# The last hidden block of both feed-forward stages in buffers of its own, and accumulator banks opened by a flag

## The chip, the cores and the metric

One Trainium2 chip, one of its cores. The time is the device time of one execution in microseconds: 890.45 us is the median of 3 runs (890.37 to 890.51). The inputs are drawn once; nothing is computed on the host.

## The reference

A block of three stages and then two attention layers, on 256 tokens of width 1024, all in float32. What the change touches is the feed-forward stage, which comes twice in the first block (`f` = 0 and `f` = 1):

```python
def swiglu(n, w_gate, w_up, w_down):
    return (jax.nn.silu(n @ w_gate) * (n @ w_up)) @ w_down

mod = (jax.nn.silu(c) @ w_ada[l] + b_ada[l])[:, None, :]
sh1, sc1, gt1, sh2, sc2, gt2, sh3, sc3, gt3 = jnp.split(mod, N_MOD, axis=-1)
n = modulate(rmsnorm(h, g_ffn1[l]), sh1, sc1)
h = h + 0.5 * gt1 * swiglu(n, w1_gate[l], w1_up[l], w1_down[l])
n = modulate(rmsnorm(h, g_mix[l]), sh2, sc2)
h = h + gt2 * hybrid_mixer(n, w_in[l], w_pool[l], pool_scale[l], w_out[l])
n = modulate(rmsnorm(h, g_ffn2[l]), sh3, sc3)
h = h + 0.5 * gt3 * swiglu(n, w2_gate[l], w2_up[l], w2_down[l])
return rmsnorm(h, g_final)
```

The inner width is 2816. After this block come a sliding-window and a block-sparse attention layer (each with its own in and out projection) and a last norm.

## The kernel before, in words

Activations lie transposed: features on the partitions, 256 tokens along the free axis. A product in float32 accuracy is made of three passes in fp32r: each operand is split into a high part (`whi`, `nhi`, `hhi`: a copy rounded to fp32r) and a low part (`wlo`, `nlo`, `hlo`: the rest), and `split_product` issues hi·hi, hi·lo and lo·hi into one accumulator.

**Weights.** They come as units of 128 x 2048 (1 MB) into three slots of `raw`. SyncE issues the load when the unit that had the slot has its low part (`lo_done`). ScalarE makes `whi` (L554), VectorE makes `wlo` (L815); each engine does its units in a written order.

**A feed-forward stage** has 11 blocks of 256 inner columns. Block i needs three units: gate, up and down. `gate` and `up` are 48 matmuls each into `sc[0]` and `sc[1]`; ScalarE takes the silu of the first into `tmp` (L721), VectorE multiplies it with the second (the hidden product, L1025), ScalarE copies the hidden block into `hhi` (L726) and VectorE writes the rest into `hlo` (L1029). `down` is 48 matmuls that add the block's part into the four banks `acc`, eight chunks m of two steps n. The banks are opened before the loop by four matmuls of a zero tile (L1441); all matmuls of `down` add only. TensorE's order in loop step j is gate j+1, up j+1, down j, so that the work on hidden block j+1 lies beside down j; `hhi` and `hlo` exist once, so `hidden_high` of block j+1 waits until down j has read them (`ffn_used`). After the last step down 10 stands alone behind down 9:

```python
act.wait_ge(ffn_used, 3 * j + (done + 4))
high(u + 4, reps=j)
act.wait_ge(ffn_used, 3 * j + (done + 5))
hidden_high(1, reps=j)
high(u + 5, reps=j)
```

**Modulation.** In the first stage each loop step also carries one unit of `w_ada`: GpSimd multiplies it by c (L467, 128 x 2048), VectorE sums it (`reduce_products`, L867) into `macc`, TensorE sums over the partitions (`mod_sum`, L1164, two matmuls) and VectorE adds the bias (`mod_out`, L876). Unit 19 is the last one needed for the first stage's own end: `mod_sum(19)` stands inside down 10 behind chunk 5. GpSimd's next unit, 20, belongs to the mixer.

**The end of a stage.** VectorE, behind its last `low`, `mod_out` and `reduce_products`, computes `gate_h` and then the residual, chunk by chunk (L829); ScalarE squares each chunk (L565), GpSimd adds the squares of chunks 0 to 3 (L476), and TensorE sums that over the partitions (L1145) between chunks 6 and 7 of down 10, then chunks 4 to 7. Standard deviation, reciprocal and the next norm follow one behind the other.

The work between the stages is ordered by lists written out by hand (`mixer_plan`); the change leaves them as they are.

## Time and profile before

| | |
|---|---|
| median of 3 runs | 890.45 us |
| the profiled execution, its own time | 890.89 us |
| span of its profile | 889.1 us |
| TensorE busy | 753.8 us, 85% |
| VectorE busy | 618.1 us, 70% |
| ScalarE busy | 403.1 us, 45% |
| GpSimd busy | 164.4 us, 18% |
| mean granted TensorE clock | 0.926 |

The first feed-forward loop runs from 69 to 246 us of the span, the second from 433 to 607 us; in both TensorE is busy without a break. Below PE is TensorE, PEld its weight loads, DVE VectorE, ACT ScalarE, POOL GpSimd, SPq SyncE's queue. L815 is line 815 of the kernel. In brackets behind a row stands the idle time before it and what ended it.

### The profile page before, as it was taken

How to read it: one execution, taken by the hardware profiler on the slowest of the kernel's cores; microseconds unless marked ns; L12 is line 12 of the kernel's file. 1: busy time of each engine (PE TensorE's matmuls, PEld its weight loads, DVE VectorE, ACT ScalarE, POOL GpSimd, SP SyncE). 2: the span in 40 equal slices, each digit the busy share in tenths (PEclk: the TensorE clock that was granted, in tenths of full speed). 3: DMA queues.
4: the chain of work that ended last, by engine and by line, in shares of the span. 5: the costliest groups of instructions: out<-in, count | busy, mean ns of one | idle time of the engine just before them, and what ended most of it. 6: DMA issues, size and time to landing. Idle time of an engine off the chain costs nothing.

```text
span 889.1 us, 14391 instructions
## 1 busy us (share of the span) xinstructions
PE 753.8 (85%) x5800; PEld 713.9 (80%) x5800; DVE 618.1 (70%) x775; ACT 403.1 (45%) x645; POOL 164.4 (18%) x87
## 2 busy tenths in 40 slices
PE   4269999999968957746999999997698979889985
PEld 3269999999957946646999999996687768878874
DVE  4987787887777978777548658545667774667741
ACT  5453343433336655442534333445366554465542
POOL 3521213322353641334002100000100000000000
PEclk9569999999978988687999999999799999999998
DMA  9877778577662963066457654654132344333201
GB/s 296 276 239 239 240 242 266 196 244 248 230 210 71 307 214 114 29 213 237 142 188 237 202 178 152 224 189 142 48 95 95 99 136 140 104 112 124 95 1 47
DMA packets 132452, 152.56 MB, mean 172 GB/s; under 512 B 2617, under 2 KB 126269, under 8 KB 132285
## 3 DMA queue, kind: packets, MB, share of 16 engines
q1 hardware_dynamic: 132324, 152.01, 52.6%
q8 instruction: 26, 0.43, 0.2%
q14 instruction: 14, 0.11, 0.0%
q10 hardware_dynamic: 88, 0.02, 0.0%
HBM read 150.97 MB, written 1.05 MB: 171 GB/s over the span
## 4 chain that ended last, share of the span: by engine, by line
PE 65%; DVE 16%; ACT 8%; issue 6%; DMA 3%; POOL 1%; SPq 0%; DVEq 0%; ACTq 0%; POOLq 0%
PE sc L1134 10%; PE sc L1136 9%; PE sc L1135 9%; PE acc L1134 8%; PE acc L1135 8%; PE acc L1136 8%; DVE macc L867 6%; ACT whi L554 2%; DVE wlo L815 2%; DMA ada<-in_w_ada_dram 2%; PE stat L1145 2%; ACT prob L656 1%; DVE rstd L835 1%; DVE prob L947 1%; DVE prob L927 1%
## 5 line engine op out<-in xcount | busy, mean ns | idle before, releaser
L815 DVE TENSOR_TENSOR wlo<-raw,whi 128x2048 fp32r<-128x2048 f32 x104 | 263.6, 2537 | 110.2 <-ACT whi L554 110.2
L554 ACT ACTIVATE whi<-raw 128x2048 fp32r<-128x2048 f32 x105 | 199.9, 1905 | 81.7 <-PE sc L1136 77.6
L1134 PE MATMUL sc<-nhi,whi 128*128 128x256 f32 x704 | 202.9, 288 | 10.1 <-DVE nlo L854 6.3
L1135 PE MATMUL sc<-nlo,whi 128*128 128x256 f32 x704 | 201.5, 286 | 0.0
L1136 PE MATMUL sc<-nhi,wlo 128*128 128x256 f32 x704 | 201.4, 286 | 0.0
L1134 PEld LDWEIGHTS sc<-nhi,whi 128*128 128x128 f32 x704 | 137.6, 196 | 10.7 <-issue 6.7
L467 POOL TENSOR_TENSOR ada<-ada,cT 128x2048 f32<-128x2048 f32 x21 | 94.4, 4497 | 255.7 <-DMA ada<-in_w_ada_dram 255.7
L1135 PEld LDWEIGHTS sc<-nlo,whi 128*128 128x128 f32 x704 | 137.7, 196 | 0.0
L1136 PEld LDWEIGHTS sc<-nhi,wlo 128*128 128x128 f32 x704 | 137.5, 195 | 0.0
L1134 PE MATMUL acc<-nhi,whi 128*128 128x256 f32 x376 | 115.0, 306 | 16.5 <-DVE nlo L854 12.1
L867 DVE TENSOR_REDUCE macc<-ada 128x256 f32<-128x2048 f32 x32 | 121.0, 3808 | 5.7 <-POOL ada L467 3.4
L1135 PE MATMUL acc<-nlo,whi 128*128 128x256 f32 x376 | 110.0, 292 | 0.0
L1136 PE MATMUL acc<-nhi,wlo 128*128 128x256 f32 x376 | 109.6, 292 | 0.0
L1134 PE MATMUL acc<-hhi,whi 128*128 128x256 f32 x352 | 100.9, 287 | 4.1 <-DVE hlo L1029 4.1
L1135 PE MATMUL acc<-hlo,whi 128*128 128x256 f32 x352 | 100.1, 284 | 0.0
L1136 PE MATMUL acc<-hhi,wlo 128*128 128x256 f32 x352 | 100.1, 284 | 0.0
L1134 PEld LDWEIGHTS acc<-nhi,whi 128*128 128x128 f32 x376 | 75.5, 201 | 24.5 <-issue 17.4
L1135 PEld LDWEIGHTS acc<-nlo,whi 128*128 128x128 f32 x376 | 76.0, 202 | 0.5 <-issue 0.5
L1136 PEld LDWEIGHTS acc<-nhi,wlo 128*128 128x128 f32 x376 | 75.8, 201 | 0.0
L1134 PEld LDWEIGHTS acc<-hhi,whi 128*128 128x128 f32 x352 | 67.4, 192 | 4.5 <-DVE wlo L815 2.6
L1135 PEld LDWEIGHTS acc<-hlo,whi 128*128 128x128 f32 x352 | 67.4, 191 | 0.1
L1136 PEld LDWEIGHTS acc<-hhi,wlo 128*128 128x128 f32 x352 | 67.3, 191 | 0.0
(164 smaller groups left out, 1168.7 us busy)
## 6 DMA issues: line engine op xcount, KB each, us to landing
ada<-in_w_ada_dram SPq DMA_DIRECT2D x32, 1024.0 KB, 5.1
raw<-in_w_gate_dram SPq DMA_DIRECT2D x22, 1024.0 KB, 5.7
raw<-in_w_up_dram SPq DMA_DIRECT2D x22, 1024.0 KB, 5.3
raw<-in_w_down_dram SPq DMA_DIRECT2D x22, 1024.0 KB, 4.9
raw<-in_w_out_dram SPq DMA_DIRECT2D x12, 1024.0 KB, 5.0
raw<-in_w_in_b_dram SPq DMA_DIRECT2D x10, 1024.0 KB, 5.0
raw<-in_w_in_a_dram SPq DMA_DIRECT2D x9, 1024.0 KB, 5.3
raw<-in_w_in_dram SPq DMA_DIRECT2D x8, 1024.0 KB, 7.8
```

Source lines behind the costliest of these rows:

```text
L467: nc.gpsimd.tensor_tensor(to, to, c_mul, ALU.mult).then_inc(prod_done, 1)
L554: nc.scalar.activation(whi[:, u % NS], raw[:, u % NS], ACT.Copy).then_inc(hi_done, 1)
L656: ins = nc.scalar.activation(prob[:, s, lo:up], prob[:, s, lo:up], ACT.Exp, bias=nm[:, s, b:b + 1], accum_out=den[:, s, b:b + 1])
L815: nc.vector.tensor_tensor(wlo[:, u % NS], raw[:, u % NS], whi[:, u % NS].bitcast(F32), ALU.subtract).then_inc(lo_done, 1)
L835: link(nc.vector.reciprocal(rstd[:, :], std[:, :]))
L867: nc.vector.tensor_reduce(macc[:, slot], src.rearrange("p c n -> p n c"), AX_X, ALU.add).then_inc(macc_done, 1)
L927: ins = nc.vector.tensor_tensor_reduce(out=prob[:, s, lo:up], in0=sc[h % 2][:, lo:up], in1=mask[:, lo:up], scale=1.0, scalar=NEG, op0=ALU. ...
L947: ins = nc.vector.tensor_scalar(prob[:, s, lo:up], prob[:, s, lo:up], rden[:, s, b:b + 1], None, ALU.mult)
L1134: mm(to, stat_hi, mov_hi, start=first, stop=False, skip_group_check=True)
L1135: mm(to, stat_hi, mov_lo, start=False, stop=False, skip_group_check=True)
L1136: return mm(to, stat_lo, mov_hi, start=False, stop=last, skip_group_check=True)
L1145: mm(ss_ps, ones[:, :], src, start=first, stop=last).then_inc(ss_done, 1)
```

## The change

Four things, the same for both stages:

- **Last block in its own buffers.** The hidden block 10 goes to `yhi[:, 0:2]` and `ylo[:, 0:2]`, which are otherwise used in the mixers (`hid_hi[1]`, `hid_lo[1]`). For it ScalarE's `hidden_high` no longer waits for down 9, and it stands ahead of the `high` of unit base+33. VectorE's `hidden_low` moves ahead of the `low` of that unit.
- **Last loop step written out** on ScalarE and VectorE (the loops end one step earlier).
- **Banks opened by a flag.** The first matmul of down 0 into each bank has `start` set; the four matmuls with the zero tile, the tile `zero_r` and its memset on GpSimd go.
- **First loop step written out** on TensorE, since the flag is set only there.

```diff
@@ -258,6 +257,8 @@
         cos1, sin1 = consts[:, C_COS:C_COS + S], consts[:, C_SIN:C_SIN + S]
         silu_g = tmp[:, 0:2, 0:S]
         hidden = tmp[:, 2:4, 0:S]
+        hid_hi = [hhi, yhi[:, 0:2]]
+        hid_lo = [hlo, ylo[:, 0:2]]
 
         start_slots = [ada[:, 0], ada[:, 1]] + [raw[:, n, :].rearrange("p (c n) -> p c n", c=DC) for n in (2, 0, 1)]
         c_mul = cT[:, :].unsqueeze(2).to_broadcast([P, DC, UC])
...
@@ -721,9 +721,9 @@
                     nc.scalar.activation(silu_g, sc[0][:, :].rearrange("p (b n) -> p b n", b=2),
                                          ACT.Silu).then_inc(silu_done, 1)
 
-                def hidden_high(i, reps=None):
+                def hidden_high(i, reps=None, buf=0):
                     act.wait_ge(hid_done, n0 + i + 1 + (reps if reps is not None else 0))
-                    nc.scalar.activation(hhi[:, :, :], hidden, ACT.Copy).then_inc(hhi_done, 1)
+                    nc.scalar.activation(hid_hi[buf][:, :, :], hidden, ACT.Copy).then_inc(hhi_done, 1)
 
                 act.wait_ge(ffn_used, done + 1)
                 silu(0)
...
@@ -731,8 +731,8 @@
                 act.wait_ge(ffn_used, done + 2)
                 high(base + 4)
                 hidden_high(0)
-                with act.Fori(0, FB - 1) as j:
-                    u = base + 2
+                u = base + 2
+                with act.Fori(0, FB - 2) as j:
                     act.wait_ge(ffn_used, 3 * j + (done + 3))
                     silu(1, reps=j)
                     high(u + 3, reps=j)
...
@@ -741,6 +741,15 @@
                     act.wait_ge(ffn_used, 3 * j + (done + 5))
                     hidden_high(1, reps=j)
                     high(u + 5, reps=j)
+                n = FB - 2
+                act.wait_ge(ffn_used, 3 * n + done + 3)
+                silu(n + 1)
+                high(u + 3 * n + 3)
+                act.wait_ge(ffn_used, 3 * n + done + 4)
+                hidden_high(n + 1, buf=1)
+                high(u + 3 * n + 4)
+                act.wait_ge(ffn_used, 3 * n + done + 5)
+                high(u + 3 * n + 5)
 
                 load_sqrt(FFN_NORM[f] + 1)
                 squares(FFN_NORM[f] + 1)
...
@@ -1024,9 +1033,9 @@
                         dve.wait_ge(hlo_done, n0 + i + add)
                     nc.vector.tensor_tensor(hidden, silu_g, up_ps, ALU.mult).then_inc(hid_done, 1)
 
-                def hidden_low(i, reps=None):
+                def hidden_low(i, reps=None, buf=0):
                     dve.wait_ge(hhi_done, n0 + i + 1 + (reps if reps is not None else 0))
-                    nc.vector.tensor_tensor(hlo[:, :, :], hidden, hhi[:, :, :].bitcast(F32),
+                    nc.vector.tensor_tensor(hid_lo[buf][:, :, :], hidden, hid_hi[buf][:, :, :].bitcast(F32),
                                             ALU.subtract).then_inc(hlo_done, 1)
 
                 low(base + 3)
...
@@ -1057,6 +1066,17 @@
                         mod_out(32)
                         reduce_products(34)
                         reduce_products(35)
+                n = FB - 2
+                u = base + 2 + 3 * n
+                low(u + 3)
+                dve.wait_ge(ffn_used, 3 * n + done + 4)
+                hidden_product(n + 1)
+                hidden_low(n + 1, buf=1)
+                low(u + 4)
+                low(u + 5)
+                if f == 0:
+                    mod_out(9 + n, 1)
+                    reduce_products(10 + n)
                 if f == 1:
                     mod_out(34)
                     dve.wait_ge(mod_done, MOD_UNITS)
...
@@ -1422,26 +1442,34 @@
                         pe.wait_ge(hid_done, n0 + i + add)
                     project(sc[1], u % NS).then_inc(ffn_used, 1)
 
-                def down(u, i, reps=None):
+                def down(u, i, reps=None, buf=0):
                     add = reps if reps is not None else 0
                     hi, lo = rows2(whi, u % NS), rows2(wlo, u % NS)
+                    first = reps is None and i == 0
                     pe.wait_ge(lo_done, u + 1 + 3 * add)
                     pe.wait_ge(hlo_done, n0 + i + 1 + add)
                     for m in range(DC):
                         for n in range(2):
                             at = slice(m * P, (m + 1) * P)
                             ins = split_product(acc[m // 2][:, (m % 2) * S:(m % 2 + 1) * S], hi[:, n, at], lo[:, n, at],
-                                                hhi[:, n], hlo[:, n], False, False)
+                                                hid_hi[buf][:, n], hid_lo[buf][:, n],
+                                                first and m % 2 == 0 and n == 0, False)
                         yield m, ins
 
                 gate(base, 0, norm=k)
                 up(base + 1, 0)
 
-                for bank in acc:
-                    mm(bank[:, :], zero_r[:, 0:P], zero_r[:, :], start=True, stop=False, skip_group_check=True)
                 if f == 0:
                     mod_sum(8, mod1_ps[:, 0:2])
-                for start, end in ((0, FB - 1),) if f == 0 else ((0, 3), (3, FB - 1)):
+                gate(base + 2, 1)
+                up(base + 3, 1)
+                for m, ins in down(base + 4, 0):
+                    if m == DC - 1:
+                        ins.then_inc(ffn_used, 1)
+                if f == 0:
+                    pe.wait_ge(mod_done, 9)
+                    mod_sum(9, mod1_ps[:, 0:2])
+                for start, end in ((1, FB - 1),) if f == 0 else ((1, 3), (3, FB - 1)):
                     with pe.Fori(start, end) as j:
                         gate(base + 2, 1, reps=j)
                         up(base + 3, 1, reps=j)
...
@@ -1454,7 +1482,7 @@
                     if end == 3:
                         mod_sum(32, mod1_ps[:, 0:2])
                         mod_sum(33, mod1_ps[:, 2:4])
-                for m, ins in down(base + 32, FB - 1):
+                for m, ins in down(base + 32, FB - 1, buf=1):
                     ins.then_inc(delta, 1)
                     if f == 0 and m == 5:
                         mod_sum(19, mod2_ps[:, 0:2])
```

The changed kernel's lines are shifted by 9 to 32 against those of before (L815 is L824 there, L867 is L876, L1029 is L1038, L1134 is L1154, L1164 is L1184).

On ScalarE, in the last loop step and behind it, the order was (`tmp<-sc` is the silu, `whi` a unit's high part, `hhi` the hidden block's high part):

```order
L721 ACTIVATE tmp<-sc 128x2x256 [waits hid_done]
L554 ACTIVATE whi<-raw 128x2048 [waits landed2]
L554 ACTIVATE whi<-raw 128x2048 [waits landed0]
L726 ACTIVATE hhi<-tmp 128x512 [waits hid_done]
L554 ACTIVATE whi<-raw 128x2048 [waits landed1]
L569 ACT_TABLE_LOAD
```

and is now, behind the loop's end:

```order
L721 ACTIVATE tmp<-sc 128x2x256 [waits hid_done,ffn_used]
L554 ACTIVATE whi<-raw 128x2048 [waits landed2]
L726 ACTIVATE yhi<-tmp 128x512 [waits hid_done,ffn_used]
L554 ACTIVATE whi<-raw 128x2048 [waits landed0]
L554 ACTIVATE whi<-raw 128x2048 [waits landed1,ffn_used]
L569 ACT_TABLE_LOAD
```

The copy of the hidden block has passed one copy of a weight unit; its `ffn_used` is now that of up 10, and the wait for down 9 stands at the last `whi`.

On VectorE the last loop step of the first stage and what follows it was (`tmp<-tmp,sc` is the hidden product):

```order
L815 TENSOR_TENSOR wlo<-raw,whi 128x2048 [waits hi_done]
L1025 TENSOR_TENSOR tmp<-tmp,sc 128x2x256 [waits hlo_done]
L815 TENSOR_TENSOR wlo<-raw,whi 128x2048 [waits hi_done]
L1029 TENSOR_TENSOR hlo<-tmp,hhi 128x512 [waits hhi_done]
L815 TENSOR_TENSOR wlo<-raw,whi 128x2048 [waits hi_done]
L876 TENSOR_TENSOR mod<-stat,biasT 128x2
L867 TENSOR_REDUCE macc<-ada 128x256 [waits mod_cols,prod_done]
L1066 TENSOR_SCALAR gate_h<-mod 128x8 [waits mod_done]
L829 SCALAR_TENSOR_TENSOR hT<-acc,gate_h,hT 128x256 [waits delta,dve_step]
```

and is now:

```order
L824 TENSOR_TENSOR wlo<-raw,whi 128x2048 [waits hi_done]
L1034 TENSOR_TENSOR tmp<-tmp,sc 128x2x256 [waits hlo_done,silu_done,ffn_used]
L1038 TENSOR_TENSOR ylo<-tmp,yhi 128x512 [waits hhi_done]
L824 TENSOR_TENSOR wlo<-raw,whi 128x2048 [waits hi_done] x2
L885 TENSOR_TENSOR mod<-stat,biasT 128x2 [waits mod_cols]
L876 TENSOR_REDUCE macc<-ada 128x256 [waits mod_cols,prod_done]
L1086 TENSOR_SCALAR gate_h<-mod 128x8 [waits mod_done]
L838 SCALAR_TENSOR_TENSOR hT<-acc,gate_h,hT 128x256 [waits delta,dve_step]
```

The hidden block's low part has passed one `wlo`; two `wlo` now follow each other, and what is behind them keeps its order.

## Rows read from the trace of the kernel before

**Rows 1.** The page, part 5: busy us, mean ns of one, idle before.

```profile
L1134 PE MATMUL acc<-hhi,whi 128*128 128x256 f32 x352 | 100.9, 287 | 4.1 <-DVE hlo L1029 4.1
```

**Rows 2.** TensorE waits, end of stage 1: total us, times, longest.

```profile
PE sc L1164 <- DVE macc L867: 3.1, 1, 3.1
PE stat L1145 <- POOL std L476: 2.6, 1, 2.6
PE acc L1134 <- DVE hlo L1029: 2.5, 1, 2.5
```

**Rows 3.** TensorE waits, end of stage 2.

```profile
PE acc L1134 <- DVE hlo L1029: 1.6, 1, 1.6
PE stat L1145 <- POOL std L476: 1.4, 1, 1.4
```

**Rows 4.** TensorE in order of time: start us, us, what; start of both loops.

```profile
68.20 1.09 PE L1441 MATMUL acc<-zero_r 128*128 128x512 f32 x4
...
69.14 0.50 PE L1164 MATMUL stat<-ones,macc 128*128 128x1 f32 x4
...
433.03 1.09 PE L1441 MATMUL acc<-zero_r 128*128 128x512 f32 x4
```

**Rows 5.** ScalarE in order of time, end of stage 1.

```profile
246.01 0.63 ACT L726 ACTIVATE hhi<-tmp 128x512 fp32r<-128x512 f32 x1 [3.78 <-PE acc L1136]
...
246.55 1.90 ACT L554 ACTIVATE whi<-raw 128x2048 fp32r<-128x2048 f32 x1
```

**Rows 6.** VectorE in order of time, end of stage 1.

```profile
224.60 2.29 DVE L815 TENSOR_TENSOR wlo<-raw,whi 128x2048 fp32r<-128x2048 f32 x1 [1.16 <-ACT whi L554]
...
240.41 0.69 DVE L1025 TENSOR_TENSOR tmp<-tmp,sc 128x512 f32<-128x512 f32 x1 [1.14 <-PE sc L1136]
...
242.26 5.73 DVE L815 TENSOR_TENSOR wlo<-raw,whi 128x2048 fp32r<-128x2048 f32 x1 [1.16 <-ACT whi L554]
...
247.92 0.68 DVE L1029 TENSOR_TENSOR hlo<-tmp,hhi 128x512 fp32r<-128x512 f32 x1
...
248.52 5.69 DVE L815 TENSOR_TENSOR wlo<-raw,whi 128x2048 fp32r<-128x2048 f32 x1
...
254.20 3.61 DVE L867 TENSOR_REDUCE macc<-ada 128x256 f32<-128x2048 f32 x1
...
257.92 2.44 DVE L829 SCALAR_TENSOR_TENSOR hT<-acc,gate_h,hT 128x256 f32<-128x256 f32 x6
```

**Rows 7.** GpSimd in order of time, same place.

```profile
224.65 5.71 POOL L467 TENSOR_TENSOR ada<-ada,cT 128x2048 f32<-128x2048 f32 x1 [11.95 <-DMA ada<-in_w_ada_dram]
...
242.24 3.60 POOL L467 TENSOR_TENSOR ada<-ada,cT 128x2048 f32<-128x2048 f32 x1 [11.88 <-DMA ada<-in_w_ada_dram]
...
248.26 3.79 POOL L467 TENSOR_TENSOR ada<-ada,cT 128x2048 f32<-128x2048 f32 x1 [2.42 <-DMA ada<-in_w_ada_dram]
```

**Rows 8.** A sum on VectorE beside a product on GpSimd.

```profile
42.04 3.65 DVE L867 TENSOR_REDUCE macc<-raw 128x256 f32<-128x2048 f32 x1
...
43.60 3.60 POOL L467 TENSOR_TENSOR ada<-ada,cT 128x2048 f32<-128x2048 f32 x1 [0.27 <-DMA ada<-in_w_ada_dram]
```

**Rows 9.** ScalarE, VectorE and GpSimd in order of time, end of stage 2.

```profile
607.78 1.90 ACT L554 ACTIVATE whi<-raw 128x2048 fp32r<-128x2048 f32 x1
...
612.32 1.66 DVE L829 SCALAR_TENSOR_TENSOR hT<-acc,gate_h,hT 128x256 f32<-128x256 f32 x4
...
614.61 1.59 POOL L476 TENSOR_TENSOR std<-std,sq 128x256 f32<-128x256 f32 x2
```

**Rows 10.** Stretches: us, busy of PE, PEld, DVE, ACT, POOL, granted clock.

```profile
249.65:253.20 3.55, 3.55 (x20) 3.55 (x19) 3.55 (x1) 0.30 (x2) 2.41 (x1) 0.52 0.23 72
...
262.00:268.00 6.00, 5.36 (x16) 4.24 (x16) 1.95 (x5) 1.28 (x3) 4.22 (x5) 0.60 1.10 349
...
614.86:620.00 5.14, 3.41 (x16) 2.40 (x16) 1.08 (x3) 1.60 (x5) 1.19 (x2) 1.00 0.36 125
```

**Rows 11.** A low part of VectorE that met a product, pool mixer.

```profile
385.81 4.13 DVE L815 TENSOR_TENSOR wlo<-raw,whi 128x2048 fp32r<-128x2048 f32 x1 [2.29 <-ACT whi L554]
```

## What the change was predicted to do

> **What bounds the kernel now.** I read the page's groups first. The product of the hidden block (`acc<-hhi,whi`, 352 matmuls of each pass) has 4.1 us of idle time before it, put down to the low part of the hidden block [rows 1]. That is what the change is aimed at, so the next view was who TensorE waits for at the end of each stage. In stage 1 the 2.5 us for `hlo` is one of three waits in 20 us: behind it stand 3.1 us for the sum `macc` of unit 19 and 2.6 us for GpSimd's sum of squares [rows 2]. In stage 2 there are 1.6 us for `hlo` and 1.4 us for the sum of squares [rows 3]. The reader is to see that TensorE waits again behind both waits that the change takes away. So the question is not when down 10 starts, but when VectorE reaches the residual, since squares, sums, deviation and the next norm hang on it one by one. For that the views in order of time were needed, engine by engine. Inside the two loops TensorE is never idle, so what goes from its stream there is gained until the loop's end.
>
> **The zero tile.** Four matmuls of 128x512 start at 68.20 us and the next instruction at 69.14, so a group costs 0.94 us of TensorE's stream; the same four stand in stage 2 at 433.03 [rows 4]. In both places the silu and the hidden product of block 0 have a whole gate product (5.7 us) ahead of the next need for them, so nothing else is late. The flagged matmul is one that was issued anyway. Gain 2 x 0.94 = 1.9 us. The memset and the `set_done` count are at the kernel's start, off every chain: 0.
>
> **Steps written out.** The same instructions in the same number; the loops' first and last passes ran through code for the first time before too, and TensorE's start-to-start time at a loop's back edge was that of straight code within a few hundredths. 0; the other end of the bound is below, with the slower case.
>
> **End of stage 1.** TensorE could start down 10 about 2.5 us earlier. I follow VectorE, in the time of the old trace (all of it shifts by 0.94 us alike). The hidden product ends at 240.41 + 0.69 = 241.10 [rows 6]. ScalarE now does the hidden copy at once, 0.63 us long, and then the unit copy of 1.9 us [rows 5], which issue 0.54 us apart: 241.16 and 241.70, ready at 241.8 and 243.6. VectorE's `hlo` runs 241.83 to 242.5. GpSimd's product starts at 242.24 [rows 7].
>
> Here the trace shows what decides. The `wlo` of 242.26 took 5.73 us and that of 248.52 took 5.69, where the one of 224.60 took 2.29 [rows 6]; GpSimd's product of 242.24 took 3.60, and that of 224.65, begun 0.05 us behind a `wlo`, 5.71 [rows 7]. Of a `wlo` and a product whichever begins second stands still until the first is done. A third case is 248.26: the product was asked for while `hlo` ran, had the next turn, and the `wlo` behind `hlo` paid.
>
> So in the changed kernel: product 19 waits for `hlo` and ends at 242.5 + 3.46 = 246.0; the first `wlo` (asked for at 243.65) ends 2.15 us behind it, as that of 242.26 did, at 248.1. ScalarE's last high part now starts when down 9 is done, 246.0, and not behind the hidden copy at 246.55 [rows 5]: it is ready at 247.9. The last `wlo` therefore starts at about 248.07, 0.45 us before its old 248.52. Product 20 starts when its data land, 248.26 [rows 7]. VectorE is first, by 0.2 us. Then the last `wlo` takes 2.29 us and not 5.69, and ends at 250.4; `mod_out` and the sum of unit 19 follow (3.61 us there [rows 6], up to 0.3 more in the loop), and the residual starts at 254.1 to 254.4 in place of 257.92. Gain 3.5 to 3.85, taken 3.7. GpSimd's product 20, pushed to 250.4 to 253.8, is over before the first squares (about 255).
>
> If product 20 is first after all, the last `wlo` ends at 254.0, and the stage gains 0.2 us. These are the two ends of this term: 0.2 and 3.85. The sum over unit 19 would then lie beside product 20; does it meet the same lock? A sum of 3.65 us at 42.04 lies over a product that began at 43.60 and took its usual 3.60 [rows 8], so no.
>
> The Trainium skill, page "SBUF — State Buffer", section "Who interferes with whom", has the rule: a two-input operation of VectorE and a GpSimd operation that reads SBUF exclude each other for the whole instruction, the first to issue wins, and `tensor_reduce` never takes part. By that rule the start order alone gives the whole 3.7 us or nothing, with no case between; the rows here show the order decided at distances of 0.02 us and 0.05 us, and none with this margin, so I keep both cases. By the rule alone the sum would be the 5.2 us below.
>
> TensorE itself ends chunk 5 of down 10 at about 250.5 and waits for unit 19 some 3.5 us; that wait grows, and costs nothing by itself.
>
> **End of stage 2.** No product of GpSimd is near. ScalarE's last high part starts when down 9 is done, 607.25, and not at 607.78 behind the hidden copy [rows 9]. The last `wlo` and the residual behind it (612.32), which follow it without a gap, come 0.53 us earlier, and with them the sum of squares that ended at 616.20 [rows 9]. So of TensorE's 1.6 us [rows 3] only 0.5 arrives; the rest turns into a longer wait for GpSimd's `std`, 1.4 + 1.6 - 0.5 = 2.5 us (2.8 by the starts).
>
> **The clock.** The idle 2.5 us before down 10 in stage 1 [rows 2] was followed by a stretch of 3.55 us at clock 0.52; in stage 2, after 1.6 and 1.4 us, the clock stayed at 1.00 [rows 10]. The new wait of 2.5 to 2.8 us is on the side of the first. Chunk 7 and the sums of squares behind it would then run at 1.2 GHz and not 2.4. Bounds: 0 if the clock stays, 3.55 x 0.48 = 1.7 us if a whole such stretch falls on work of the chain. I take the middle, 0.9. In stage 1 the same place ran at 0.60 already [rows 10], so nothing is lost there, and the slow stretch of down 10 goes without a gain, because down 10 is no longer on the chain.
>
> **Sum.** 1.9 + 3.7 + 0.5 - 0.9 = 5.2 us off the profiled execution's own 890.89, or 885.7. The median of the runs is 0.44 below the profiled execution, so 885.2 us. It rests on the pool mixer passing on the shift: there each load waits for a `wlo` or a sum of VectorE that shifts with it, and the units that it needs first have been loaded long before.
>
> **Rivals.**
> - *GpSimd keeps the turn.* Product 20 lands or issues before the last `wlo`. For it: the margin of 0.2 us is within what a landing can vary, and twice in the rows above the order hung on less. Against it: all the terms of the margin shift together. Gain 1.9 + 0.2 + 0.5 - 0.9 = 1.7: 889.2, as a median 888.8 us.
> - *Both waits for `hlo` go in full.* 2.5 + 1.6 + 1.9 = 6.0: 884.5 us. Against it: the later waits in rows 2 and 3, which this case needs to shift by themselves.
> - *Slower: a new collision between the stages.* The pool mixer has several products of GpSimd and `wlo`s of VectorE that land next to each other; at 385.81 one `wlo` took 4.13 us [rows 11] and not 2.29. After a shift that is not the same for both (product 20 and unit 21 are moved by another amount than the chain), one more `wlo` on the chain can meet a whole product, at 5.73 - 2.29 = 3.4 us. Together with the first rival that is 1.7 - 3.4: 892.2 us. It decides only from an extra 1.7 us on (5.2 us if VectorE had its turn). Against it: the loads there are ordered by VectorE's own events, so most pairs keep their distance. A late code fetch of the parts written out would act the same way; nothing in TensorE's rows at the loops shows one.
> - *Other mixes*, such as the first case without the clock's cost (884.3) or a part of the shift lost in the pool mixer (886 to 888).
>
> **How the numbers follow.** The forecast 0.52, GpSimd keeps the turn 0.27, both waits in full 0.04, a new collision 0.07, other mixes 0.10. A difference under 0.2%, 1.8 us, can't be told from none here. The forecast, the full waits, nearly all mixes and some of the first rival (with the clock cost at 0 it is 887.9) are faster: 0.73. Same: the rest of the first rival and little else, 0.20. Slower: 0.07. The range goes from 884.0 (the forecast with the clock's cost at 0 and its term at 3.85) to 889.4 (the first rival with the clock's cost at 1.7 and a little less).
>
> **What would show it.** In the profile after: no `zero_r`, and each loop 0.94 us earlier; TensorE goes from down 9 into down 10 without a wait in both stages; the last `wlo` of stage 1 about 2.3 us long (right) or 5.5 (the first rival); a wait for `macc` of 3 to 4 us in stage 1 (7 in the rival); in stage 2 a wait for `std` of 2.5 to 2.8 us, and behind it the granted clock at one of its two levels. It would be wrong if VectorE were not what the residual waits for in either stage, or if the distance between the two stages' starts (about 365 us between the zero tiles) changed by more than the end of stage 1 gained.

## The result, and the profile after

| | before | after |
|---|---|---|
| time, median (lowest to highest) | 890.48 us (890.37 to 891.11, 4 runs) | 884.12 us (883.01 to 884.97, 4 runs) |
| after / before, 95% interval | | 0.9926 (0.9909 to 0.9944) |
| span of the profiled execution | 889.1 us | 881.2 us |
| its own time | 890.89 us | 883.01 us |
| mean granted TensorE clock | 0.926 | 0.922 |

The ratio makes 883.9 us of the 890.45: 6.6 us gained, where 5.2 was forecast. The direction held, and so did the steps at the change's own places; the time by the ratio lies 0.1 us below the range of 884.0 to 889.4. Parts that the change doesn't touch moved too.

The page's group of the last hidden product no longer has its 4.1 us of idle time [rows 1]: of its matmuls, those from `hhi` have none before them.

```profile
L1154 PE MATMUL acc<-hhi,whi 128*128 128x256 f32 x320 | 90.1, 281 | 0.0
```

TensorE's waits at the end of stage 1 and of stage 2, in the changed kernel (total us, times, longest), answer to [rows 2] and [rows 3]:

```profile
PE sc L1184 <- DVE macc L876: 3.3, 1, 3.3
PE stat L1165 <- POOL std L477: 1.8, 1, 1.8
```

```profile
PE stat L1165 <- POOL std L477: 2.7, 1, 2.7
```

Both waits for the hidden block's low part are gone, and what stood behind them is what TensorE waits for: 3.3 us for unit 19's sum and 1.8 for the sum of squares in stage 1, and in stage 2 the sum of squares with 2.7 us in place of 1.4.

TensorE in order of time (start, us, instruction), at the start of loop 1 and from down 9 into down 10, answers to [rows 4]:

```profile
67.30 0.28 PE L1156 MATMUL sc<-nhi,wlo 128*128 128x256 f32 x1
67.42 0.50 PE L1184 MATMUL stat<-ones,macc 128*128 128x1 f32 x4
67.78 0.36 PE L1154 MATMUL sc<-nhi,whi 128*128 128x256 f32 x1
...
243.90 0.28 PE L1156 MATMUL acc<-hhi,wlo 128*128 128x256 f32 x1
244.02 0.50 PE L1184 MATMUL stat<-ones,macc 128*128 128x1 f32 x4
244.38 0.36 PE L1154 MATMUL acc<-yhi,whi 128*128 128x256 f32 x1
...
252.17 0.49 PE L1184 MATMUL sc<-ones,macc 128*128 128x1 f32 x3 [3.31 <-DVE macc L876]
```

No zero tile stands between up 0 and the sum of unit 8, and down 10 (`acc<-yhi`) follows down 9 without a break. But it then stands still from 248.9 to 252.17, until unit 19 is there.

ScalarE, VectorE and GpSimd in order of time around down 10 of stage 1 [rows 5 to 7], a fence for each:

```profile
239.30 0.64 ACT L726 ACTIVATE yhi<-tmp 128x512 fp32r<-128x512 f32 x1 [4.14 <-DVE tmp L1034]
239.84 1.90 ACT L554 ACTIVATE whi<-raw 128x2048 fp32r<-128x2048 f32 x1
244.22 1.92 ACT L554 ACTIVATE whi<-raw 128x2048 fp32r<-128x2048 f32 x1 [2.48 <-PE acc L1156]
```

```profile
239.97 0.69 DVE L1038 TENSOR_TENSOR ylo<-tmp,yhi 128x512 fp32r<-128x512 f32 x1 [0.76 <-ACT yhi L726]
241.77 6.71 DVE L824 TENSOR_TENSOR wlo<-raw,whi 128x2048 fp32r<-128x2048 f32 x2 [1.11 <-ACT whi L554]
...
248.47 3.65 DVE L876 TENSOR_REDUCE macc<-ada 128x256 f32<-128x2048 f32 x1
252.23 2.44 DVE L838 SCALAR_TENSOR_TENSOR hT<-acc,gate_h,hT 128x256 f32<-128x256 f32 x6
```

```profile
240.53 3.60 POOL L468 TENSOR_TENSOR ada<-ada,cT 128x2048 f32<-128x2048 f32 x1 [11.88 <-DMA ada<-in_w_ada_dram]
246.55 5.39 POOL L468 TENSOR_TENSOR ada<-ada,cT 128x2048 f32<-128x2048 f32 x1 [2.42 <-DMA ada<-in_w_ada_dram]
```

The reader is to see whose turn it is. Product 19 (240.53) makes the first `wlo` wait; the two `wlo` from 241.77 take 6.71 us together, where those of 242.26 and 248.52 took 5.73 and 5.69 [rows 6]. The second of them starts at 246.20. Product 20 comes at 246.55, 0.35 us behind it, and this time it is the product that stands still (5.39 us against 3.79). The residual starts at 252.23 in place of 257.92.

VectorE at the end of stage 2 [rows 9]:

```profile
600.76 2.29 DVE L824 TENSOR_TENSOR wlo<-raw,whi 128x2048 fp32r<-128x2048 f32 x1 [2.10 <-ACT whi L554]
...
603.36 2.44 DVE L838 SCALAR_TENSOR_TENSOR hT<-acc,gate_h,hT 128x256 f32<-128x256 f32 x6
609.61 0.88 DVE L838 SCALAR_TENSOR_TENSOR hT<-acc,gate_h,hT 128x256 f32<-128x256 f32 x2 [3.80 <-PE acc L1156]
```

And the stretches in which I read the clock (us, busy of PE, PEld, DVE, ACT, POOL, granted clock): stage 1 from `gate_h` to the reciprocal, and the end of stage 2 [rows 10]:

```profile
252.04:261.44 9.40, 6.85 (x26) 5.56 (x26) 4.52 (x13) 3.60 (x9) 6.56 (x8) 0.64 0.93 293
604.50:612.60 8.10, 4.85 (x17) 3.83 (x16) 2.20 (x7) 3.02 (x9) 2.17 (x3) 0.79 0.37 126
```

**Where the time went.** VectorE has one hidden product for each block, one `gate_h` for each stage and one reciprocal for each norm. The times between their starts cut a profile into parts that can be laid beside those of another kernel. Worked out from these rows of each profile, in us:

| kernel | start | loop 1 | end 1 | norm 1 | mixer | loop 2 | end 2 | norm 2 | attention |
|---|---|---|---|---|---|---|---|---|---|
| before | 68.40 | 172.01 | 17.32 | 10.25 | 148.49 | 168.42 | 10.46 | 8.25 | 262.22 |
| after | 67.62 | 170.90 | 13.52 | 9.40 | 147.57 | 167.33 | 10.05 | 9.42 | 262.11 |
| after, again (f1) | 67.70 | 169.14 | 13.60 | 10.13 | 148.27 | 167.33 | 10.05 | 9.43 | 262.17 |
| flag alone (e1) | 67.39 | 170.64 | 17.29 | 10.33 | 148.59 | 167.51 | 10.46 | 8.25 | 262.23 |
| buffers alone (e2) | 68.14 | 171.40 | 13.55 | 10.50 | 148.56 | 168.25 | 10.04 | 9.34 | 262.49 |
| before, product held (e3) | 68.59 | 171.57 | 14.12 | 9.48 | 148.01 | 168.42 | 10.47 | 8.24 | 261.44 |
| after, product first (e4) | 68.11 | 170.90 | 17.49 | 9.39 | 147.04 | 167.33 | 10.04 | 9.44 | 261.95 |
| after, product held (g3) | 67.52 | 170.90 | 13.56 | 9.39 | 147.34 | 167.34 | 10.04 | 9.42 | 262.52 |
| after, gap filled (f2) | 67.15 | 170.46 | 13.52 | 10.49 | 148.63 | 167.33 | 10.05 | 8.28 | 266.03 |
| after, 8 more (g1) | 67.25 | 170.33 | 13.52 | 10.34 | 148.67 | 168.29 | 10.05 | 10.58 | 265.97 |
| after, 16 more (g2) | 66.91 | 170.50 | 13.61 | 10.36 | 148.52 | 169.25 | 10.04 | 8.25 | 262.48 |
| `wlo` later (f3) | 67.60 | 170.49 | 11.50 | 10.30 | 148.54 | 167.34 | 8.13 | 8.65 | 262.28 |
| and product 19 on ScalarE (f4) | 67.51 | 170.35 | 10.28 | 8.28 | 147.97 | 167.33 | 8.14 | 8.67 | 265.17 |

Between the mixer and loop 2 (the rest of the norm ahead of stage 2, and gate and up of its block 0) lie 16.74 to 16.77 us in all (16.60 in f4), left out here. Loop is from the first to the eleventh hidden product, end from there to `gate_h`, norm from there to the next reciprocal (norm 1 and norm 2 are those behind stage 1 and stage 2); attention is all behind the reciprocal of norm 2, to the last sum.

From before to after the parts sum to 7.90 us, which is the distance of the two profiled executions (7.88). The change's own places give 1.11 + 3.80 + 1.09 + 0.41 = 6.41. Norm 2 takes back 1.17. The rest, 2.66 us, comes from the start (0.78), norm 1 (0.85), the mixer (0.92) and the attention (0.11), none of which the change touches.

Two of these can be followed to rows. In norm 1 the last sums of squares of TensorE take less time; the first row is of the kernel before, the second of the changed one:

```profile
264.15 3.21 PE L1145 MATMUL stat<-sq,ones 128*128 128x256 f32 x8
```

```profile
258.47 2.36 PE L1165 MATMUL stat<-sq,ones 128*128 128x256 f32 x8
```

The difference is 0.85 us, all that norm 1 gained. The granted clock of the last 3 us of norm 1 was 0.69 in the kernel before and 0.84 in the changed one, where a low stretch ended sooner. In the mixer the difference lies in its first 14.4 us, before and after:

```profile
267.98:282.38 14.40, 10.92 (x70) 10.95 (x71) 10.65 (x18) 8.19 (x12) 1.51 (x3) 0.76 0.07 16
```

```profile
261.44:275.84 14.40, 10.92 (x79) 10.95 (x79) 11.55 (x19) 9.16 (x14) 2.49 (x3) 0.88 0.14 38
```

TensorE has 79 matmuls in them in place of 70; one takes 0.41 us where the clock is low and 0.28 where it isn't.

### The profile page after: what moved, and what is told of

Read it like the earlier page. It is cut to its first block, busy times and chain, and to the rows that moved or that the text cites. A ratio compares the mean times of both kernels' runs of the same rounds, so it can differ in the third digit from the quotient of the medians.

```text
span 881.2 us, 14334 instructions
## 1 busy us (share of the span) xinstructions
PE 752.3 (85%) x5792; PEld 713.0 (81%) x5792; DVE 609.0 (69%) x775; ACT 403.3 (46%) x645; POOL 169.5 (19%) x86
## 4 chain that ended last, share of the span: by engine, by line
PE 66%; DVE 16%; ACT 8%; issue 6%; DMA 2%; POOL 1%; SPq 0%; DVEq 0%; POOLq 0%; ACTq 0%
PE sc L1154 10%; PE sc L1155 10%; PE sc L1156 10%; PE acc L1154 8%; PE acc L1155 8%; PE acc L1156 8%; DVE macc L876 6%; ACT whi L554 2%; DVE wlo L824 2%; PE stat L1165 2%; DMA ada<-in_w_ada_dram 2%; ACT prob L656 1%; DVE rstd L844 1%; DVE prob L956 1%; DVE prob L936 1%
## 5 line engine op out<-in xcount | busy, mean ns | idle before, releaser
L824 DVE TENSOR_TENSOR wlo<-raw,whi 128x2048 fp32r<-128x2048 f32 x104 | 252.4, 2430 | 107.5 <-ACT whi L554 107.5
L1154 PE MATMUL sc<-nhi,whi 128*128 128x256 f32 x704 | 203.0, 288 | 10.1 <-DVE nlo L863 6.5
L468 POOL TENSOR_TENSOR ada<-ada,cT 128x2048 f32<-128x2048 f32 x21 | 99.6, 4743 | 250.5 <-DMA ada<-in_w_ada_dram 250.5
L1154 PEld LDWEIGHTS sc<-nhi,whi 128*128 128x128 f32 x704 | 137.7, 196 | 10.8 <-issue 6.9
L1154 PE MATMUL acc<-nhi,whi 128*128 128x256 f32 x376 | 114.5, 305 | 16.5 <-DVE nlo L863 12.1
L876 DVE TENSOR_REDUCE macc<-ada 128x256 f32<-128x2048 f32 x32 | 121.0, 3807 | 5.9 <-POOL ada L468 3.4
L1154 PEld LDWEIGHTS acc<-nhi,whi 128*128 128x128 f32 x376 | 75.0, 200 | 24.5 <-issue 17.4
L1155 PE MATMUL acc<-hlo,whi 128*128 128x256 f32 x320 | 90.1, 282 | 0.0
L1154 PE MATMUL acc<-hhi,whi 128*128 128x256 f32 x320 | 90.1, 281 | 0.0
L1156 PE MATMUL acc<-hhi,wlo 128*128 128x256 f32 x320 | 90.0, 281 | 0.0
L1184 PE MATMUL sc<-ones,macc 128*128 128x1 f32 x92 | 18.2, 307 | 49.5 <-DVE macc L876 39.9
L1155 PEld LDWEIGHTS acc<-hlo,whi 128*128 128x128 f32 x320 | 60.3, 188 | 0.0
L1154 PEld LDWEIGHTS acc<-hhi,whi 128*128 128x128 f32 x320 | 60.3, 188 | 0.0
```

Of the source, the lines that this page charges most:

```text
L468: nc.gpsimd.tensor_tensor(to, to, c_mul, ALU.mult).then_inc(prod_done, 1)
L824: nc.vector.tensor_tensor(wlo[:, u % NS], raw[:, u % NS], whi[:, u % NS].bitcast(F32), ALU.subtract).then_inc(lo_done, 1)
L876: nc.vector.tensor_reduce(macc[:, slot], src.rearrange("p c n -> p n c"), AX_X, ALU.add).then_inc(macc_done, 1)
L1154: mm(to, stat_hi, mov_hi, start=first, stop=False, skip_group_check=True)
L1155: mm(to, stat_hi, mov_lo, start=False, stop=False, skip_group_check=True)
L1156: return mm(to, stat_lo, mov_hi, start=False, stop=last, skip_group_check=True)
```

## The experiments

My theory: the gain at stage 1's end comes from the order of turns between GpSimd's product 20 and VectorE's last `wlo`, not from down 10 starting earlier; each loop gains the zero tile; the rest is the clock. The rival: the waits for `hlo` are themselves the gain. The kernels e1 to e4, f1 to f4 and g1 to g3 ran in three groups, each on one chip with the kernel before beside it (889.05, 890.05 and 889.25 us there). A first time is a median, and the ratio is to the kernel before in the same group with its 95% interval; across groups only ratios and parts are compared.

**e1, the flag alone.** The changed kernel without its buffers and without the written-out last step.

```diff
-                for bank in acc:
-                    mm(bank[:, :], zero_r[:, 0:P], zero_r[:, :], start=True, stop=False, skip_group_check=True)
...
-                                                hhi[:, n], hlo[:, n], False, False)
+                                                hhi[:, n], hlo[:, n],
+                                                first and m % 2 == 0 and n == 0, False)
```

> The kernel before with the banks opened by the flag and the first loop step written out on TensorE; the last hidden block stays in hhi and hlo. If the zero tiles cost what their starts say, both loops start 0.94 us earlier and nothing else moves: 1.9 us off, about 888.6 us, with 2.5 and 1.6 us of wait for hlo still there. Rival, the flag gave more (a shift of 4 us or more, because stage 1's end is met at another time): under 887 us.

Measured: 887.26 us (885.64 to 890.07, 12 runs), ratio 0.9984 (0.9969 to 0.9998). That is 1.4 us off by the ratio, where 1.9 was expected, and its interval, 0.2 to 2.8 us, holds both. The parts are clearer: loop 2 is shorter by 0.91 us and loop 1 by 1.37 (the untouched start by 1.0), the two ends are as before (17.29, 10.46). The zero tile's price is that of [rows 4], 0.94.

**e2, the buffers alone.** The changed kernel with the zero tile and TensorE's loop as before.

```diff
-                with act.Fori(0, FB - 1) as j:
+                with act.Fori(0, FB - 2) as j:
...
+                hidden_high(n + 1, buf=1)
+                high(u + 3 * n + 4)
```

> The changed kernel with the zero tiles and the loops of before on TensorE. Theory of the turn: all but 1.9 us of the change's gain is here, 885.5 to 886.5 us, with the last low part of stage 1 about 2.3 us long and GpSimd's product 20 over 5 us. Rival, the removed waits themselves are the gain: the same time, but then the residual of stage 2 starts 1.6 us or more earlier against its loop's end, and not 0.5.

Measured: 887.18 us (882.11 to 891.31, 12 runs), ratio 0.9981 (0.9963 to 0.9999), above the 885.5 to 886.5 expected. End 1 is 3.77 us shorter, end 2 0.42, and norm 2 1.09 longer. The last `wlo` of stage 1 takes 2.28 us and product 20 5.37, as the theory of the turn had it. Loop 2 is 0.17 us shorter with the same TensorE instructions: in the written-out last step the hidden product starts 0.04 us behind the last matmul of up, in the passes of the loop 0.21. That term I had put at 0. The locals are those of the whole change, yet e1 and e2 gain 1.4 and 1.7 us as ratios and the whole 6.6. So the totals don't add, though the parts do (ends, loop 2 and norm 2), and something outside them moves the total by a few us.

**e3, the old buffers with product 20 held** until the last `wlo` is done.

```diff
+            pool.wait_ge(lo_done, FFN_UNIT[0] + 3 * FB + 2)
             product(20)
```

> The kernel before with one wait added: GpSimd holds the product of unit 20 until VectorE's last low part of stage 1 is done. Buffers and zero tiles as before. Theory of the turn: the last low part falls from 5.7 to 2.3 us and the residual of stage 1 starts 3.4 us earlier, so 3.4 us off, 887.0 us, though TensorE still waits 2.5 us for hlo. Rival, the wait for hlo sets the end of stage 1: no change, 890.5 us.

Measured: 885.19 us (884.38 to 887.24, 6 runs), ratio 0.9959 (0.9943 to 0.9975), or 3.7 us off where 3.4 was expected. TensorE's waits in this kernel, and VectorE and GpSimd in order of time:

```profile
PE stat L1146 <- POOL std L476: 2.6, 1, 2.6
PE acc L1135 <- DVE hlo L1030: 2.5, 1, 2.5
```

```profile
248.23 2.28 DVE L816 TENSOR_TENSOR wlo<-raw,whi 128x2048 fp32r<-128x2048 f32 x1
...
250.50 3.85 DVE L868 TENSOR_REDUCE macc<-ada 128x256 f32<-128x2048 f32 x1
...
254.47 0.88 DVE L830 SCALAR_TENSOR_TENSOR hT<-acc,gate_h,hT 128x256 f32<-128x256 f32 x2
```

```profile
242.11 5.65 POOL L467 TENSOR_TENSOR ada<-ada,cT 128x2048 f32<-128x2048 f32 x1 [14.21 <-DMA ada<-in_w_ada_dram]
250.59 3.60 POOL L467 TENSOR_TENSOR ada<-ada,cT 128x2048 f32<-128x2048 f32 x1 [2.83 <-DVE wlo L816]
```

The wait for `hlo` is still 2.5 us, and end 1 is 3.20 us shorter all the same: the last `wlo` takes 2.28 us and not 5.69, and the wait for `macc` is gone. The rival falls: 3.20 of the 3.80 us of stage 1 are had with the wait left in. In this profile product 19 also lost its turn (a `wlo` started at 242.01, the product at 242.11), but so it did in e1, whose end 1 is as before.

**e4, the changed kernel with the old order of turns**, forced by a wait of VectorE.

```diff
                 low(u + 4)
+                if f == 0:
+                    dve.wait_ge(prod_done, products(20, False))
                 low(u + 5)
```

> The changed kernel, but VectorE's last low part of stage 1 waits until GpSimd's product of unit 20 is done, the order that the kernel before had. Theory of the turn: it starts at about 250.1 us of the span and not at 246.2, so 3.7 to 4.0 us slower than the changed kernel, about 888 us. Rival, the new buffers are what brings the gain: at most 1 us slower than the changed kernel, 885 us.

Measured: 887.45 us (884.49 to 889.84, 12 runs), ratio 0.9982 (0.9969 to 0.9995). TensorE's wait, and VectorE's last `wlo`:

```profile
PE sc L1186 <- DVE macc L876: 7.3, 1, 7.3
```

```profile
242.27 4.54 DVE L824 TENSOR_TENSOR wlo<-raw,whi 128x2048 fp32r<-128x2048 f32 x1 [1.11 <-ACT whi L554]
250.72 2.29 DVE L824 TENSOR_TENSOR wlo<-raw,whi 128x2048 fp32r<-128x2048 f32 x1 [3.91 <-POOL ada L468]
```

End 1 is 17.49 us, 3.97 longer than in the changed kernel (3.7 to 4.0 expected) and 0.17 longer than before. Down 10 starts as early as in the changed kernel and stands still for 7.3 us. This is the forecast's rival "GpSimd keeps the turn", which was priced at 888.8 us; the ratio makes 888.8 of the 890.45. With e3 it shows both halves: order without buffers gives 3.2 us, buffers without order none. Of the last 0.6 of the 3.80, 0.4 is the new buffers' too: the last `wlo` starts 7.68 us behind the hidden product in the changed kernel and 8.07 in e3. The other 0.2 is the sum into `macc`, 3.85 us in e3 and 3.65 in the changed kernel.

**g3, the changed kernel with product 20 held**, by the same line as e3.

```diff
+            pool.wait_ge(lo_done, FFN_UNIT[0] + 3 * FB + 2)
             product(20)
```

> The changed kernel with GpSimd's product 20 held until the last low part of stage 1 is done, so that VectorE has its turn whatever the landing. The profiles of the changed kernel show it so already: the same time within 1 us. If in some unprofiled runs the product had been first (the 2 us between its runs), the slower of them go, and the median falls by 1 us or more.

Measured: 883.12 us (881.7 to 884.83, 7 runs), ratio 0.9941 (0.9919 to 0.9964). End 1 is 13.56 us, as without the wait (13.52). The margin on which the forecast hung, put at 0.2 us, was 0.35 and 0.36 in the two profiles of the changed kernel, and enough; a wait that makes sure of it has no cost that these runs show.

**f1, the changed kernel once more**, with no edit.

> The changed kernel once more, for its spread. If the 884.1 us of its first runs is the mechanisms' sum, it stands 5 to 6.5 us below the kernel before again. Rival, part of it was the luck of four runs (where the slow stretches of TensorE's clock and the first loads happened to fall): 4 us or less below the kernel before, single runs 2 us apart or more.

Measured: 883.43 us (882.74 to 884.31, 5 runs), ratio 0.9926 (0.9912 to 0.9939). Ends, loop 2 and norm 2 repeat to 0.1 us. Norm 1 doesn't (10.13 against 9.40), nor the mixer (148.27 against 147.57) nor loop 1 (169.14 against 170.90): of the 2.66 us from untouched parts, which part gives them changes from run to run. The 1.76 us of loop 1 are no clock inside it: its granted clock is 1.00 in all thirteen profiles. They lie between its first two hidden products (12.14 us in the first profile, 10.38 here); the distances of the others agree to 0.02 us. What differed was the stretch ahead of them, first the changed kernel's first profile and then this one:

```profile
58.00:66.00 8.00, 6.95 (x37) 6.96 (x38) 8.00 (x4) 2.10 (x2) 0.00 (x0) 0.57 0.72 276
```

```profile
58.00:66.00 8.00, 6.31 (x52) 6.17 (x52) 8.00 (x4) 2.92 (x4) 0.00 (x0) 1.00 0.69 250
```

At a clock of 1.00 in place of 0.57 TensorE entered the loop further on in its work. In norm 1 and at the mixer's head this profile is as the kernel before: 3.09 us for the last sums of squares, and a clock of 0.76.

**f2, the new gap of stage 2 filled** with 22 matmuls whose results nobody reads.

```diff
+                    if f == 1 and m == 6:
+                        for n in range(22):
+                            mm(sc[1][:, 0:S], hid_hi[1][:, 0, 0:P], hid_hi[1][:, 0], start=True, stop=True)
```

> The changed kernel with 22 matmuls of no use in TensorE's wait for GpSimd's sum of squares at the end of stage 2 (they write a free bank). If the idle 2.7 us there is what lets the clock fall, chunk 7 and the sums behind it run at full clock: that part 1.2 us shorter, the whole 0.5 to 1.2 us below the changed kernel. Rival, the clock falls or not whatever is put there: the same time.

Measured: 887.49 us (886.35 to 888.77, 7 runs), ratio 0.9973 (0.9962 to 0.9984). TensorE in the gap, and the stretch's clock in f2 and then in the changed kernel:

```profile
605.66 2.80 PE L1494 MATMUL sc<-yhi 128*128 128x256 f32 x22
608.57 0.70 PE L1165 MATMUL stat<-std,ones 128*128 128x256 f32 x2
```

```profile
605.60:612.70 7.10, 6.27 (x40) 5.06 (x39) 2.35 (x7) 3.18 (x9) 2.22 (x3) 1.00 0.46 143
```

```profile
605.60:612.70 7.10, 4.76 (x16) 3.83 (x16) 1.20 (x4) 2.13 (x6) 1.45 (x2) 0.76 0.30 103
```

The clock stays at 1.00 where it was 0.76, and norm 2 is 1.14 us shorter. So that cost is the clock, as the forecast said: TensorE did nothing for 2.7 us and the work behind came at the lower level, 1.2 GHz, for part of it. But the whole came out 4.1 us slower than f1 on the same chip. The stretch from the fifth reciprocal to the sixth, in the attention layers, which is the same in both kernels, shows where, in f2 and then in the changed kernel:

```profile
622.72:750.38 127.66, 112.86 (x844) 99.58 (x844) 82.47 (x217) 65.87 (x150) 2.20 (x3) 0.93 0.32 105
```

```profile
622.24:747.15 124.91, 109.70 (x844) 96.77 (x844) 82.54 (x216) 65.87 (x150) 2.22 (x3) 0.96 0.33 107
```

It has the same 844 matmuls and takes 2.75 us longer at a clock of 0.93 in place of 0.96. The gain at one place came with a larger loss at another. Whether the filler brought that loss isn't shown: g1, which has none in the gap, has the same 127.6 us there, and norm 1 and the mixer, ahead of the filler, are 1.1 us longer each than in the changed kernel's first profile.

**g1 and g2, 8 and 16 more matmuls** ahead of loop 2 of the changed kernel, for nobody, to shift all behind them.

```diff
+                if f == 1:
+                    for n in range(8):
+                        mm(acc[n % 4][:, 0:S], nhi[:, n % 8, 0:P], nhi[:, n % 8], start=True, stop=True)
```

> The changed kernel with 8 matmuls of no use (256 columns, 0.12 us each) behind the second product of stage 2, where its zero tiles stood: 0.95 us more work in a stretch at full clock. If times add up, 1 us slower than the changed kernel, 884.8 us. If what comes behind also depends on where it falls against TensorE's slow stretches, the parts behind stage 2 differ from the changed kernel's by up to 2 us either way though nothing in them is changed.

> The same with 16 matmuls, 1.9 us. If times add up, 1.9 us slower than the changed kernel, 885.7 us. If the slow stretches matter, another amount, and not twice that of the kernel with 8: as the kernel with the new buffers and the old zero tiles, which had 1.9 us more work and came out about 4 us slower.

Measured: g1 887.79 us (881.66 to 891.38, 12 runs), ratio 0.9977 (0.9955 to 1.0); g2 885.3 us (882.89 to 891.84, 12 runs), ratio 0.9968 (0.9949 to 0.9987). Loop 2 is longer by exactly 0.96 and 1.92 us. Against g3 on the same chip the medians of g1 and g2 are 4.7 and 2.2 us higher, the ratios 3.2 and 2.4: the whole doesn't follow the work added. That the smaller addition cost more isn't shown, since the intervals of g1 and g2 overlap. The end of stage 2 in g1 and then in g2:

```profile
604.50:612.60 8.10, 5.40 (x30) 4.84 (x29) 4.01 (x11) 2.52 (x7) 2.18 (x3) 0.75 0.53 167
```

```profile
604.50:612.60 8.10, 5.24 (x38) 4.52 (x36) 4.90 (x11) 3.39 (x10) 2.18 (x3) 1.00 0.63 200
```

With the same wait ahead of it (2.7 us in each), norm 2 takes 10.58 us in g1 at a clock of 0.75, 8.25 in g2 at 1.00, and 9.42 in the changed kernel at 0.79; the attention layers take 265.97, 262.48 and 262.11. So what the clock did behind the same wait was not the same in three profiles, which reached the end of stage 2 (`gate_h`) at 603.2, 605.2 and 605.9 us of the span. The 12 runs of either spread over 9 us and more, the 4 and 5 of the changed kernel's two sets over 2; but the kernel before, unchanged, spread over 7.4 us in its 24 runs beside them, so the spread isn't shown to come from the added matmuls.

**f3, the last `wlo` of each stage behind the residual.** Down 10 needs unit base+32; base+33 and base+34 are the next stage's, and VectorE splits both ahead of the residual. Here base+34 waits until the residual is done (in stage 1 until the norm is), and product 20 until the sums of squares are; the two edits are not told apart.

```diff
-            product(20)
             add_squares(1)
+            product(20)
...
                 low(u + 4)
-                low(u + 5)
...
                 residual(FFN_NORM[f] + 1)
+                if f == 1:
+                    low(base + 34)
...
             normalise(1)
+            low(FFN_UNIT[0] + 3 * FB + 1)
```

> The changed kernel with the last low part of each stage moved behind the residual (stage 1: behind the norm; stage 2: right behind the residual), and GpSimd's product 20 behind the sums of squares. If VectorE's order is what the ends of both stages wait for, the residual starts 2.2 us earlier in each, and TensorE's waits for macc and std shrink by as much: 3.5 to 5 us below the changed kernel. Rival, the moved low parts come back as a wait of the first projections of the mixer: 2 us or less below it.

Measured: 879.66 us (879.1 to 880.97, 4 runs), ratio 0.9883 (0.9868 to 0.9898). VectorE in stage 1 and TensorE's waits there and in stage 2:

```profile
241.34 4.59 DVE L824 TENSOR_TENSOR wlo<-raw,whi 128x2048 fp32r<-128x2048 f32 x1 [1.11 <-ACT whi L554]
...
245.93 3.74 DVE L876 TENSOR_REDUCE macc<-ada 128x256 f32<-128x2048 f32 x1
...
249.78 2.44 DVE L838 SCALAR_TENSOR_TENSOR hT<-acc,gate_h,hT 128x256 f32<-128x256 f32 x6
```

```profile
PE stat L1167 <- POOL std L477: 2.6, 1, 2.6
PE sc L1186 <- DVE macc L876: 1.3, 1, 1.3
```

```profile
PE stat L1167 <- POOL std L477: 0.9, 1, 0.9
```

End 1 is 2.0 us shorter and end 2 1.9 than in the changed kernel: nearly the 2.29 us of the `wlo` taken out. So the residual hangs on what VectorE does ahead of it, in both stages, as the forecast held. Against f1 on the same chip the kernel is 3.8 us faster (3.5 to 5 expected).

**f4, f3 with product 19 on ScalarE** (`by_act`), so that GpSimd has none beside the last `wlo` left.

```diff
-    return (a < MOD_START or 20 <= a < 32) and a % 2 == 1 or a == 22
+    return (a < MOD_START or 20 <= a < 32) and a % 2 == 1 or a in (19, 22)
...
+                if f == 0:
+                    product(19)
```

> As the kernel before this one, and the product of unit 19 is made by ScalarE and not by GpSimd, so that VectorE's low part behind the hidden block meets no product. That low part then takes 2.3 us and ends 2.1 us earlier, the sum of unit 19 starts when the product is ready (245.0 in the changed kernel's span and not 246.3): 1.0 to 1.5 us below the kernel before this one. Rival, ScalarE's last high part, pushed back by the product, is needed: the same or slower.

Measured: 877.97 us (876.11 to 879.05, 4 runs), ratio 0.9857 (0.9841 to 0.9872). VectorE and ScalarE in stage 1:

```profile
241.11 2.29 DVE L826 TENSOR_TENSOR wlo<-raw,whi 128x2048 fp32r<-128x2048 f32 x1 [1.11 <-ACT whi L554]
...
244.31 3.91 DVE L878 TENSOR_REDUCE macc<-ada 128x256 f32<-128x2048 f32 x1 [0.26 <-ACT ada L591]
...
248.34 2.05 DVE L840 SCALAR_TENSOR_TENSOR hT<-acc,gate_h,hT 128x256 f32<-128x256 f32 x5
```

```profile
240.98 3.29 ACT L591 ACTIVATE ada<-ada,cT 128x256 f32<-128x256 f32 x8
```

The `wlo` of 241.11 meets nothing and takes 2.29 us in place of 4.59. The 3.29 us more of ScalarE push its last `whi` back by 0.6 us, and nothing here needs that one sooner. End 1 is 1.2 us shorter again, and norm 1 2.0 at a granted clock of 1.00 throughout; the attention layers, untouched, are 2.9 longer. This is the fastest kernel of the study: 12.7 us below the kernel before by its ratio and 5.5 below the changed kernel on the same chip (f1), with 3.3 at the end of stage 1 and 1.9 at that of stage 2.

## Why the prediction was right at the change's own places and wrong on the clock

- **The zero tile**, 2 x 0.94: right. 0.91 in loop 2 of e1; none is left in TensorE's rows.
- **Steps written out**, 0: small miss. Loop 2 gives 1.09 and not 0.91; e2 alone has the 0.17.
- **End of stage 1**, 3.7: right. 3.80, 3.72 in f1, with the row of each step where it was put: TensorE waits 3.3 us for `macc` (3 to 4 forecast), the residual comes 3.80 us earlier against the loop's end. The last `wlo` won by the order of start, 0.35 us ahead of the product where 0.2 was forecast; e3 shows that the order alone gives 3.20 of it, and e4 that there is no gain without it. The Trainium skill, page "SBUF — State Buffer", section "Who interferes with whom", has it that the first to issue holds the shared ports for the whole instruction and the other blocks fully. These runs agree: 2.28 us alone in e3, 5.69 behind a product in [rows 6], and the product pays 5.39 when it is second.
- **End of stage 2**, 0.5: right. 0.41, and the wait for `std` is 2.7 us (2.5 to 2.8 forecast).
- **The clock**, -0.9: this is the step that failed. The term priced one place, the wait at the end of stage 2, and put the clock of every other part at nothing. At its own place it was near: 1.17 us at clock 0.79, and 1.09 to 1.19 in f1, e2, e4 and g3. But for stage 1 the forecast held that it "ran at 0.60 already [rows 10], so nothing is lost there", and it named no other place. In its place the runs showed that the low stretches shift against the work: norm 1 gained 0.85 us, all in the last sums of squares (3.21 to 2.36), and the mixer 0.92 in a head that ran at 0.88 in place of 0.76. g3 and e4 repeat both (9.39 us and 0.88). In f1 they are 0.12 and 0.22, and loop 1 gained 2.87 instead of 1.11, behind a stretch at 1.00. That such parts move together with the clock's low stretches is read from rows; no run set the clock and nothing else.
- **The sum.** The terms that repeat give 6.41 - 1.17 = 5.24 us, the forecast's 5.2. The measured 6.6 (5.0 to 8.1 by its interval; 5.4 to 7.8 in f1) holds 1.4 more, which no instruction of the change explains. The first interval alone doesn't tell it from nothing; that of f1 does by 0.2 us.
- **The range.** Its lower end, "the forecast with the clock's cost at 0 and its term at 3.85", let the clock move one place by 0.9 us. It is also mis-added: 1.9 + 3.85 + 0.5 makes 884.2 us and not 884.0. In g1 and f2 the attention layers moved by 3.9 us, and one kernel's runs by up to 9. The page of the kernel before has a row that I should have counted in, the granted clock of the forty slices of its span in tenths:

```profile
PEclk9569999999978988687999999999799999999998
```

In eleven of forty it is below 0.9, most of them outside the two places that I looked at. By the parts that moved in g1 and f2, an estimate of 3 to 4 us to either side was needed.
- **The sign of being wrong** was there, and it came: the distance between the two stages' starts was to change by no more than the end of stage 1 gained. Between the first hidden products of the two stages it fell from 364.83 to 358.16 us, by 6.67, where end 1 gave 3.80 and loop 1 1.11; norm 1 and the mixer are the rest.

The rivals: "GpSimd keeps the turn" is a real kernel (e4), just not this one. "Both waits in full" gave 884.5 us, near the measured 883.9, for the wrong reason: in e3 the wait stands and the gain of its stage is there. No new collision came in the mixer, where all kernels lie between 147.0 and 148.7 us.

What stays open: why the extra 1.4 us came both times that the changed kernel ran (0.9926 twice) if it is only the clock's places, and why its 4 and 5 runs spread over 2 us where the 24 of the kernel before spread over 7. No run here held the clock at one level throughout.

## What to carry to other kernels

When a wait of the busiest engine goes, follow the engine that the chain returns to: here the gain of stage 1 was in VectorE's order behind TensorE, and the wait removed was worth nothing by itself (e4). Where a two-input operation of VectorE and a product of GpSimd come within a microsecond of each other on the chain, try to hold the one off the chain by a wait (e3: 3.2 us at the end of stage 1; g3: no cost seen), and to move whatever the next stage alone needs behind the chain's last step (f3: 3.8 us). Read a change of under 1% in the parts that it touches: the sum over untouched parts moved by as much here.

## What the runs showed of the hardware

- **The turn goes by the order of start at small distances too**: 0.35 us in the changed kernel and 0.10 in e3, `wlo` first both times. It costs the loser the winner's rest: `wlo` 2.28 to 2.29 us alone, 4.5 to 5.7 behind a product; product 3.60 alone, 5.4 to 5.7 behind a `wlo`.
- **The same idle time is not always followed by a lower clock.** About 2.7 us of TensorE's waiting at one place of the program was followed by a stretch at 0.79 (after), 0.75 (g1) or 1.00 (g2); g1 and g2 came there 2.1 and 2.8 us later in the span.
- **The low stretches shift against untouched work**: the mixer's first 14.4 us ran at 0.76 in the kernel before and in f1, at 0.88 in the changed kernel's first profile, which had 79 matmuls in them and not 70 or 71.
- **A filler kept the clock up at its own place and the kernel was slower all the same**: against the changed kernel's first profile f2 gained 1.14 us in norm 2 and lost 3.9 in the attention layers.
- **Straight code started a waiting instruction 0.17 us earlier** than the loop's last pass (loop 2 of e2, 168.25 against 168.42): 0.04 us behind the matmul that it waits for and not 0.21. The form of its waits changed with the loop, so which of the two it is isn't shown.
